# Inverting the chunk triangles of a delta-rule recurrence as 32x32 blocks in four row tiles, instead of 64x64 blocks in two

## The reference, cut to what matters

```python
def step(state, inp):
    r_t, w_t, k_t, v_t, kk_t, a_t = inp
    sa = jnp.einsum("bhvk,bhk->bhv", state, kk_t)
    state = (state * w_t[:, :, None, :]
             - sa[..., None] * (kk_t * a_t)[:, :, None, :]
             + v_t[..., None] * k_t[:, :, None, :])
    return state, jnp.einsum("bhvk,bhk->bhv", state, r_t)
```

## Time and profile before

| | us |
|---|---|
| median of 3 runs (2106.38 to 2111.42) | 2110.09 |
| span of the profiled execution | 2103.3 |
| median less span (the page gives no time of its own for the profiled execution) | 6.8 |
| recurrence stage, first to last PE work | 307.8 to 434.6 |
| its four chunks of inversion | 313.5 to 422.1 |
| PE busy, whole kernel | 2021.3 |
| DVE / ACT / POOL busy | 1079.6 / 800.6 / 135.1 |

### The profile page before, as it was taken

One profiled execution on the slowest core, in us unless ns is written; L12 is line 12 of the kernel. 1 busy time (PEld: TensorE's weight loads), 2 busy tenths in 40 slices (PEclk: granted clock), 3 DMA queues, 4 the chain that ended last, 5 costly groups with the idle time before them and its releaser, 6 DMA issues. The chain is left out here.

```text
span 2103.3 us, 29578 instructions
## 1 busy us (share of the span) xinstructions
PE 2021.3 (96%) x11736; PEld 1611.2 (77%) x11736; DVE 1079.6 (51%) x1815; ACT 800.6 (38%) x1301; POOL 135.1 (6%) x173
## 2 busy tenths in 40 slices
PE   8999879989999998999999999999999999999997
PEld 6778648868888887888888777876666788888886
DVE  5665384464444635577774254238555554423433
ACT  5432342243324424444443232326555544412421
POOL 0000136600000000000000000000000000000000
PEclk9999999999999999999999999999999999999998
DMA  4233200013232430233333423231111222232232
GB/s 177 75 117 113 85 21 3 3 66 116 92 101 91 140 120 13 90 100 98 100 93 110 167 85 105 91 100 51 41 32 40 71 93 90 99 100 92 98 100 80
DMA packets 48594, 181.96 MB, mean 87 GB/s; under 512 B 5504, under 2 KB 5888, under 8 KB 47840
## 3 DMA queue, kind: packets, MB, share of 16 engines
q1 hardware_dynamic: 44240, 165.61, 24.0%
q0 software_dynamic: 3088, 12.90, 1.8%
q10 hardware_dynamic: 1152, 1.89, 0.3%
HBM read 175.08 MB, written 5.29 MB: 86 GB/s over the span
## 5 line engine op out<-in xcount | busy, mean ns | idle before, releaser
L209 DVE TENSOR_TENSOR weights_lo<-weights_raw,weights_hi 128x1024 fp32r<-128x1024 f32 (+2 forms) x288 | 364.4, 1265 | 787.5 <-ACT weights_hi L201 787.3
L201 ACT ACTIVATE weights_hi<-weights_raw 128x1024 fp32r<-128x1024 f32 (+2 forms) x288 | 313.5, 1088 | 836.5 <-PE sp_ps L234 251.1
L232 PE MATMUL sp_ps<-arena_parts,weights_hi 128*128 128x512 f32 x720 | 284.1, 395 | 3.0 <-DVE arena_parts L303 2.5
L234 PE MATMUL sp_ps<-arena_parts,weights_lo 128*128 128x512 f32 x720 | 281.9, 392 | 0.0
L233 PE MATMUL sp_ps<-arena_parts,weights_hi 128*128 128x512 f32 x720 | 281.7, 391 | 0.0
L232 PE MATMUL end_ps<-arena_parts,weights_hi 128*128 128x512 f32 x576 | 224.9, 390 | 0.5 <-DVE arena_parts L305 0.5
L233 PE MATMUL end_ps<-arena_parts,weights_hi 128*128 128x512 f32 x576 | 224.4, 390 | 0.0
L234 PE MATMUL end_ps<-arena_parts,weights_lo 128*128 128x512 f32 x576 | 224.3, 389 | 0.0
L232 PE MATMUL fr_ps<-arena_parts,weights_hi 128*128 128x512 f32 (+1 forms) x480 | 182.3, 380 | 1.9 <-DVE arena_parts L305 1.1
L233 PE MATMUL fr_ps<-arena_parts,weights_hi 128*128 128x512 f32 (+1 forms) x480 | 180.7, 377 | 0.0
L234 PE MATMUL fr_ps<-arena_parts,weights_lo 128*128 128x512 f32 (+1 forms) x480 | 180.7, 376 | 0.0
(11 more groups left out here) (389 smaller groups left out, 3035.6 us busy)
## 6 DMA issues: line engine op xcount, KB each, us to landing
weights_raw<-w_up SPq DMA_DIRECT2D x44, 512.0 KB, 3.5
weights_raw<-w_proj SPq DMA_DIRECT2D x38, 512.0 KB, 3.5
weights_raw<-w_gates SPq DMA_DIRECT2D x32, 576.0 KB, 3.7
weights_raw<-w_ca SPq DMA_DIRECT2D x32, 512.0 KB, 3.5
weights_raw<-w_down SPq DMA_DIRECT2D x16, 704.0 KB, 4.1
weights_raw<-w_in SPq DMA_DIRECT2D x22, 512.0 KB, 3.5
weights_raw<-w_logits SPq DMA_DIRECT2D x16, 512.0 KB, 3.5
weights_raw<-w_ff1a SPq DMA_DIRECT2D x16, 512.0 KB, 3.4
```

The lines of the kernel that those rows point to most:

```text
L201: act.activation(self.w_hi[:, g % 2, 0:cols], self.raw[:, g % 2, 0:cols], ACT.Copy).then_inc(self.hi_ready, 1)
L209: dve.tensor_tensor(self.w_lo[:, g % 2, 0:cols], self.raw[:, g % 2, 0:cols], self.w_hi[:, g % 2, 0:cols].bitcast(F32), ALU.subtract).then_ ...
L232: pe.matmul(out, left[0], right[0], start=start, stop=False)
L234: return pe.matmul(out, left[1], right[0], start=False, stop=stop)
```

## The change

The diagonal blocks that are inverted by doubling are now 32x32 (SUB = 32), four to a head. POOL first packs the four diagonal 32x32 blocks of each head (`pack`, four copies for each half, each on 32 partitions) so that they stand on their own partitions in 32 columns; 4 heads are 128 columns. Levels 0 to 4 run on these: one POOL multiply of 128x128 in place of two of 64x256, ACT copies of 128x256 in place of 128x512, DVE subtractions of 128x128 in place of 128x256. On PE each group of 8 matmuls of 64x64 becomes a group of 16 matmuls of 32x32 (`quarters`), block q on rows and output partitions 32q to 32q+31.

The sixth level, which joins two 32x32 inverses into one of 64x64, is done for its 32x32 corner alone. `corner_products` turns the inverse and multiplies the Gram matrix's corner by the upper inverse (8 matmuls of 32x32 a half, in tiles off the array's diagonal). ACT's `take_corners` copies the corner products (2 operations on 32 partitions) and writes the four turned 32x32 inverses straight into the Gram matrix (4 operations on 32 partitions); the last product waits for the fourth of these six. `corner_step` makes the corner (8 matmuls a half), in the banks Z and O, and DVE's `corners` writes it with a minus sign. The solve afterwards reads the same 64x64 blocks as before.

New waits: POOL waits for its own pack before level 0; `inverse_start` and `solve_upper` wait for ACT's block copies (`blocks_ready`); `corner_step` waits for the banks Z and O; `right_side` waits for the end of the inversion between its two parts. The table of constants loses 960 columns and gains none.

```diff
-    ("neg_ones", 128), ("neg_diag_t", 128), ("level", 896), ("flip", 128),
+    ("level", 160), ("unit", 32), ("flip", 128),
...
-    LEVELS, HALF = 6, 4 * HD
+    LEVELS, SMALL, HALF, SUBS = 6, 5, 4 * HD, 4 * SUB
...
+                quarters = [(m, q) for m in range(4) for q in range(4)]
+
+                def turn_inverse(half):
+                    for m, q in quarters:
+                        pe.matmul(ps[sub_rows(q), INVERSE + half, sub_cols(m)], inv[sub_rows(q), sub_cols(4 * half + m)],
+                                  core.c("ident", q * SUB, SUB)[sub_rows(q), :], start=True, stop=True)
...
                         if n >= 2:
-                            for m in range(4):
-                                for b in range(2):
-                                    rows = block_rows(b)
-                                    pe.matmul(ps[rows, INVERSE + half, block_cols(m)], inv[rows, block_cols(4 * half + m)],
-                                              core.c("ident", b * HD, HD)[rows, :], start=True, stop=True)
-                        for m in range(4):
-                            for b in range(2):
-                                rows = block_rows(b)
-                                mm = pe.matmul(ps[rows, INVERSE + half, block_cols(4 + m)], level[g % 2][rows, block_cols(4 * half + m)],
-                                               inv[rows, block_cols(4 * half + m)], start=True, stop=True)
+                            turn_inverse(half)
+                        for m, q in quarters:
+                            mm = pe.matmul(ps[sub_rows(q), INVERSE + half, sub_cols(4 + m)],
+                                           level[g % 2][sub_rows(q), sub_cols(4 * half + m)],
+                                           inv[sub_rows(q), sub_cols(4 * half + m)], start=True, stop=True)
                         mm.then_inc(prod_done, 1)
...
+                def corner_products(ch):
+                    for half in range(2):
+                        pe.wait_ge(step_ready, 2 * (LEVELS * ch + SMALL - 1) + half + 1)
+                        turn_inverse(half)
                         for m in range(4):
                             for b in range(2):
+                                upper, lower = sub_rows(2 * b), sub_rows(2 * b + 1)
+                                mm = pe.matmul(ps[lower, X + half, sub_cols(8 + m)],
+                                               gram(ch, 4 * half + m)[upper, b * HD + SUB:b * HD + HD],
+                                               inv[upper, sub_cols(4 * half + m)], start=True, stop=True)
+                        mm.then_inc(prod_done, 1)
+
+                def corner_step(ch):
+                    for half in range(2):
+                        pe.wait_ge(prod_ready, 2 * ((LEVELS - 1) * ch + SMALL - 1) + half + 1)
+                        if ch:
+                            pe.wait_ge(out_ready if half else state_sum, ch)
+                        for m in range(4):
+                            for b in range(2):
+                                upper, lower = sub_rows(2 * b), sub_rows(2 * b + 1)
+                                mm = pe.matmul(ps[upper, (Z, O)[half], sub_cols(m)], turned[lower, half, sub_cols(4 + m)],
+                                               gram(ch, 4 * half + m)[lower, b * HD + SUB:b * HD + HD], start=True, stop=True)
                         mm.then_inc(step_done, 1)
...
+                def take_corners(ch):
+                    for half in range(2):
+                        act.wait_ge(prod_done, 2 * ((LEVELS - 1) * ch + SMALL - 1) + half + 1)
+                        for b in range(2):
+                            lower = sub_rows(2 * b + 1)
+                            act.activation(turned[lower, half, SUBS:], ps[lower, X + half, 2 * SUBS:3 * SUBS], ACT.Copy)
+                        for q in (1, 3, 0, 2):
+                            b, at = q // 2, q % 2 * SUB
+                            ins = act.activation(grams(ch, 4 * half, 4)[sub_rows(q), :, b * HD + at:b * HD + at + SUB],
+                                                 subs(ps[sub_rows(q), INVERSE + half, 0:SUBS]), ACT.Copy)
+                            if q == 3:
+                                ins.then_inc(prod_ready, 1)
+                        ins.then_inc(blocks_ready, 1)
```

More of the change, by code:

```diff
@@ L20 @@
 HD = 64
+SUB = 32
 HEADS = 8
@@ L1123, in inverse_start @@
                         if ch:
                             pe.wait_ge(step_ready, 2 * LEVELS * ch - 1 + half)
-                        for m in range(4):
-                            for b in range(2):
-                                rows = block_rows(b)
-                                mm = pe.matmul(ps[rows, INVERSE + half, block_cols(m)], level[LEVELS * ch % 2][rows, block_cols(4 * half + m)],
-                                               core.c("ident", b * HD, HD)[rows, :], start=True, stop=True)
+                            pe.wait_ge(blocks_ready, 2 * (ch - 1) + half + 1)
@@ L1130, in inverse_start @@
+                        for m, q in quarters:
+                            mm = pe.matmul(ps[sub_rows(q), INVERSE + half, sub_cols(m)],
+                                           level[SMALL * ch % 2][sub_rows(q), sub_cols(4 * half + m)],
+                                           core.c("ident", q * SUB, SUB)[sub_rows(q), :], start=True, stop=True)
                         mm.then_inc(step_done, 1)
                 def products(ch, n):
-                    g = LEVELS * ch + n
+                    g = SMALL * ch + n
@@ L1252, in _ @@
                     gram_unit(ch + 1, 0, 1)
-                    products(ch, 5)
+                    corner_products(ch)
                     gram_unit(ch + 1, 0, 2)
-                    step(ch, 5)
+                    corner_step(ch)
                     gram_unit(ch + 1, 0, 3)
@@ L1320, in _ @@
                     take_products(ch, 4)
-                    take_products(ch, 5)
+                    take_corners(ch)
                 take_upper(NT - 1)
@@ L3379, in _constants @@
     c["neg_tri"][:] = -1.0 * (row >= col)
-    c["neg_ones"][:] = -1.0
-    c["neg_diag_t"][:] = np.where(row < col, 0.0, NEG)
-    for n in range(7):
+    inner, across = i[:, None] % SUB, np.arange(SUB)[None, :]
+    for n in range(5):
         b = 1 << n
-        c["level"][:, n * P:(n + 1) * P] = (col // b % 2 == 1) & (row // b == col // b - 1)
+        c["level"][:, n * SUB:(n + 1) * SUB] = (across // b % 2 == 1) & (inner // b == across // b - 1)
+    c["unit"][:] = inner == across
     for n in range(NW):
```

88 lines of the change are left out of this document (49 added, 39 removed).

## The result

The changed kernel takes 2145.62 us, median of 4 runs (2143.73 to 2147.78); the kernel before, in 4 runs beside it, 2108.32. The ratio is 1.018, with a 95% interval of 1.016 to 1.019. The forecast was 2088, with a range to 2120: wrong in sign and outside.

What follows compares the result with a forecast made beforehand. PE, busy for 96% of the span, was taken to bound the kernel. Passes -26.9, last level +6.0, POOL -2.3 and tiling changes +1.3 sum to -21.9 us: span 2103.3 to 2081.4, time 2088, range 2081 to 2120.

Steps and rivals of the forecast that it cites:

- The step that failed: PE passes of the inversion: 58 ns in one tile, 29 in two, so array time sets the pace, not instruction issue.
- the sum's first term: PE's inversion groups: 13.9 us a chunk become 6.2 plus 1.0 for the corner, 26.9 us less in four chunks.
- The pace of 7.5 ns: 32x32 passes on PE: about 30 ns in a tile, so four tiles side by side take one every 7.5 ns.
- The line from 128 and 64 columns of weights to 32: Cost of a PE pass in a tile: doubles from 64 to 128 columns, carried down to about 30 ns at 32.
- The ring: One level's loop through PE, ACT and DVE without Gram units: 1.9 us for 3.29, 1.4 less.
- The rival that ended slower: Every pass costs PE something whatever its tile; at 22.5 ns a pass the kernel takes 2137 us; chance 0.23.
- read as a price to the whole engine: The skill page's 60 cycles of overhead a matmul, 25 ns, taken as a cost to all of PE: near 2146 us.
- ACT in the last level: Six ACT copies a half instead of one, 0.28 us each, the step waiting for four: +6.0 us together.
- POOL: One multiply of 0.45 us a level and half, pack copies 0.29 each; PE's 2.3 us of waits on POOL go.
- What the prediction named as showing it wrong: Turn groups of 0.45 us: size doesn't pay; 0.7 or more: passes have their own price; chunk-start waits: pack is dear.
- Right signs of the pace: In turn and product groups, pass starts 7 to 8 ns apart, a group of 32 passes in 0.24 us.
- From span to time: Whole kernel: 6.8 us between profiled span and median, added to the forecast span of 2081.4 to give 2088.

Runs made afterwards that it cites:

- experiment 1: Kernel before plus 384 matmuls of 32x32 and 192 of 64x64 on constants, waiting for nothing, at the stage's start: 2144.92 us, single run.
- experiment 3: Kernel before with each 64x64 matmul of the inversion issued as two of 32 moving columns: 2158.49 us, ratio 1.024.
- corner kernel: Kernel before with the changed kernel's last level (32x32 corner alone), levels 0 to 4 by 64x64: 2122.92 us, ratio 1.007.
- experiment 5: Kernel before with only the changed last level, 2122.92 us; the same with idle matmuls in PE's wait for ACT's corner copies, 2110.20 us.
- experiment 4: Kernel before with 32x32 turns and products in levels 2 and 4, 2107.31 us; levels 2 to 4, 2113.21; also steps of levels 1 to 4, 2128.05.

## Why the prediction was wrong

- **The step that failed** is the sentence "the array is the limit, not the handing out of instructions", and with it the sum's first term, 832 passes at 7.5 ns. 29 ns a pass was both limits at once: the array's, and the supply's 256 instructions in 3.6 us. Four tiles moved the first to 8.4 ns and left the second at 28. With 1792 instructions a chunk for 960 no gain of any size was to be had: the stage's 33 packets need 119 us at 3.6 us each, for 122.1 before, and that if PE never had to wait for one. In place of the 26.9 us of the first term the inversion's groups gave back 11 of busy time, and the stops cost 18.6.
- **The pace of 7.5 ns** was nearly right as a burst: 8.4 (experiment 1). The line from 128 and 64 columns of weights to 32 holds, and experiment 3 shows that the weights are its variable.
- **The ring.** A level without Gram units was to take 1.9 us; level 3 after goes from 325.76 to 330.91, 5.15, with two stops, 0.42 and 1.23, partly at half clock.
- **The rival that ended slower** gave 2137 and was the nearest, by the wrong mechanism, so its nearness is luck. It looked for an even price, and the earlier trace rows, 22.5 ns over 8 passes, could neither show nor exclude a limit that appears only over hundreds of instructions. The sentence of the Trainium skill's page "TensorEngine Tiling (Array Packing)", section "Instruction Overhead", gave 2146 read as a price to the whole engine. The number is the measured one by chance, for the reading is refuted: passes ran 8.4 ns apart, a third of the 25 ns that 60 cycles are at 2.4 GHz. The same page of the Trainium skill also advises not to take a tiling factor from a dimension that is already small. The result agrees with that in direction, 2145.62 for 2108.32, for another reason than the overhead that stands there.
- **The clock** was not in the sum at all. The working took waits at their length. In the corner kernel pauses of about 1 us, three of four, cost some 12 us more in the matmuls behind them, and the untouched matmuls of the stage took 31.6 us longer.
- **ACT in the last level**: 0.268 us a copy for 0.28. The corner in the kernel before costs 2 us with the clock held up, and 13.5 without (experiment 5): size right, consequence missed.
- **POOL**: multiply 0.454 us for 0.45, pack copy 0.286 for 0.29, and no wait at the chunk's border for the pack. The waits on POOL fell from 2.3 to 1.7 us, not to nothing.
- What the prediction named as showing it wrong (turn groups of 0.45 us or 0.7, waits at the chunk's start) did not occur as meant. Turn groups took 0.27 us at full clock (experiment 4), but 0.42 to 0.44 at half (325.76 to 326.20), which by its number is the sign for size not paying: it can be read only with the clock beside it. Right signs of the pace were seen in a kernel 37 us slower: the check list had no line for idle time without a releaser.
- **From span to time**, 6.8 us were added. In every later run the time lies 1.8 us above the span of the same execution, so some 5 of the 6.8 were the difference between two executions; nothing hangs on them.

The cause is shown, by one burst, by adding and removing instructions, by stops that stand multiples of 256 instructions apart, and by the filled corner wait. How the 37 us divide between stops and clock is not settled, since the clock falls because of the stops; the profile's sums (+20 idle, +32 slower work, -11) are a reading, not an experiment.

## What to carry to other kernels

Count TensorE's instructions against time, not only its array work: here 256 of them, 128 passes of float32, took 3.5 to 3.7 us to arrive, so a stretch of several hundred passes below 29 ns each stops, however many tiles run abreast. Read the instruction queue's packets in a dense stretch. What moved from 317 to 335.5 us, in slices of 0.46 us, before and after:

```profile
GB/s 0 35 0 0 0 0 0 0 0 0 0 0 0 35 0 0 0 0 0 0 0 0 0 0 35 0 0 0 0 0 0 0 0 0 0 35 0 0 0 0
```

```profile
GB/s 35 0 0 0 0 0 0 0 35 0 0 0 0 0 0 0 35 0 0 0 0 0 0 0 35 0 0 0 0 0 0 0 35 0 0 0 0 0 0 0
```

Before, a packet comes every 11 or 12 slices, 5.1 to 5.6 us; after, every 8, 3.7 us, which is the pace of the burst: that stretch waits for instructions. An average over the stage (6.1 us a packet before, 4.9 after) doesn't show it. And price a new pause of PE near 1 us by the matmuls behind it at half clock too, which here followed three pauses of four; if another engine sets the pause, filling it with idle matmuls may cost nothing and give several times its length.

## What the runs showed of the hardware

- Instructions arrive 256 at a time. At hand are some hundreds: in the burst 237 passes (474 instructions) ran before the first stop, which at 4.5 us was the longest, in a stretch where all queues together moved 182 GB/s. In no run did two packets start less than 3.2 us apart in the stage.
- 32x32 float32 passes in four tiles: 8.4 ns apart at full clock, 13 at half (128 in 1.7 us); 64x64 in two tiles 29 and 53.
- A pass with 64x64 weights costs 29 ns with 32 moving columns as with 64.
- The granted clock went from 1.00 (331 to 338 us) to 0.51 (338 to 344.8) behind a pause of 0.93 us, in a kernel that otherwise kept PE at work; behind a third pause of the same length it stayed at 1.00.
